# A two-layer hybrid network: eight stages of a layer written as three

## The chip, the cores and the metric

The kernel runs on one core of a Trainium2 chip. A core has a matrix engine (PE, its weight loads PEld), a vector engine (DVE), a scalar engine (ACT), a general engine (POOL) and a queue (SP) that issues transfers. The metric is the device time of one execution in microseconds, the median of the runs shown.

## What is computed

Two layers run over 640 tokens (512 latent, 128 of context) of width 1024. Of a layer, this is what the change touches:

```python
h = rmsnorm(x, lp['norm1_g']) * (1.0 + sc1) + sh1
proj = h @ lp['w_in']
r_a, k_a, v_a, q_b, k_b, v_b, x_c, g_c = jnp.split(proj, SPLIT_POINTS, axis=-1)
# differential attention: rotated queries and keys, then
o = rmsnorm(o, lp['diff_subln_g'], eps=1e-5) * (1.0 - lam_init)
# recurrence: its outputs' end
o = head_layernorm(o_sum, lp['rwkv_ln_g'].reshape(H_A, HD_A))
bonus = jnp.sum(rh * kh * lp['rwkv_rk'], axis=-1, keepdims=True) * vh
out = (o + bonus).reshape(B, T, W_A) * g
```

`sh1`, `sc1` and four more vectors come from a product of the condition with `mod_w`. Behind this follow the output projection and an expert stage, which the change leaves as they are, but for the place of the norm's squares.

## The kernel before, in words

Everything is fp32, with tokens along the free axis (`[128, chunk, 640]`). Large products split each operand into a high and a low part (`high` on ACT, `low` on DVE) and issue three matmuls (`split3`, L196 to L198). Each stage is an `nc.Block()`: each engine runs its own list in order, semaphores order them inside, and all engines meet at its end. Buffers live as long as the Python scope that holds them.

A layer's stages, in order: `load_stage` (the vectors' transfer L159, small products and exponentials); `mod_stage` (three small DVE steps, `mod_shifts`); `proj_gemm` (norm 1, then 21 columns of 128, with weights in a ring of three, PSUM in pairs of banks 0 to 5, and the linear recurrence on DVE and ACT beside it; banks 6 and 7 hold its gates); `vtok_stage` (values with tokens on the partitions: three pieces of 256 columns, five token tiles each, 15 groups of 24 matmuls, weights in one raw buffer and two split ones); `rope_stage` (eight rotations: PE permutes L871, POOL times cosine L881, DVE times sine L888 and adds L891; pieces 0 and 1 of the late modulation); `rwkv_prepare` (low-rank products L978, key norm, then four rounds of decays, and modulation pieces 2 to 7); `mix_stage` (the recurrence and the attention); `subln_stage`; `rwkv_finish`; then the output projection.

`Modulation` computes a vector piece from 2 MB of weights in two halves of a ring: `sums` (L346) and `turn` (L355) on PE, `take_row` (L363) and `take_columns` (L368) on ACT. It uses banks 5 to 7. In `rwkv_prepare` ACT handles two pieces ahead of each round's three exponentials (L1021 to L1024), on which DVE's round waits (L1063).

In `norm_programs` ACT writes squares (L456) into a ring of two, PE sums them (L479), DVE scales the sum (L484), ACT takes `Ln` and `Exp`, DVE multiplies (L494), ACT scales and makes the high part, and DVE the low one (L489). In `proj_gemm` DVE's three first `low` steps stand ahead of L484.

## Time and profile before

| | us |
|---|---|
| median of 3 runs | 4836.77 (4822.12 to 4838.63) |
| profiled execution, its own time | 4823.6 |
| its span in the profile | 4821.8 |
| matrix engine busy | 4173.8 (87%) |
| vector engine busy | 3557.3 (74%) |
| scalar engine busy | 1498.2 (31%) |
| general engine busy | 1304.8 (27%) |

The profile shows each engine's instructions with start and duration. Busy shares are means over all stages; since stages end at a common point, each is read by its own window. Clock is the granted share of the matrix engine's 2.4 GHz: 0.50 is 1.2 GHz.

### The profile page before, as it was taken

What the parts mean: (1) busy time and instruction counts of PE and PEld (TensorE: products, weight loads), DVE (VectorE), ACT (ScalarE), POOL (GpSimd) and SP (SyncE); (2) the same over time, 40 slices, a digit from 0 to 9 for tenths busy, and PEclk for the clock granted to TensorE, in tenths of its full rate; (3) what the DMA queues carried; (4) which work ended last, traced back from release to release, by engine and by line L of the source; (5) the groups of instructions that cost most, each with busy time, mean ns of one, the idle gap of its engine ahead of it and who ended that gap; (6) DMA issues with size and microseconds to landing.
All of it is one profiled execution on the core that took longest, in us unless ns stands there. A gap on an engine that the chain in (4) does not pass through costs nothing. (4 is left out here: it accounts for less than half of the span.)

```text
span 4821.8 us, 74006 instructions
## 1 busy us (share of the span) xinstructions
PE 4173.8 (87%) x28014; PEld 3382.9 (70%) x28014; DVE 3557.3 (74%) x6627; ACT 1498.2 (31%) x2206; POOL 1304.8 (27%) x1046
## 2 busy tenths in 40 slices
PE   6977996899878999999879689868996989999996
PEld 4955775875556878888768367768653777887885
DVE  2436654359997999999944466433799979999997
ACT  3323542311123333332242245223111333323333
POOL 0000000004302666655500000000133046656553
PEclk8977987999989999999989689789998999999998
DMA  5132001239968999999821400012587799999996
GB/s 210 49 123 74 2 2 37 88 95 321 300 181 301 409 408 408 403 406 404 327 70 58 161 5 2 2 51 81 190 302 239 225 350 408 408 408 405 404 407 230
DMA packets 402055, 1079.48 MB, mean 224 GB/s; under 512 B 37632, under 2 KB 177152, under 8 KB 395136
## 3 DMA queue, kind: packets, MB, share of 16 engines
q1 hardware_dynamic: 254336, 539.10, 31.7%
q0 software_dynamic: 147456, 536.94, 28.9%
q8 instruction: 157, 2.57, 0.2%
q14 instruction: 106, 0.87, 0.1%
HBM read 996.47 MB, written 79.43 MB: 223 GB/s over the span
## 5 line engine op out<-in xcount | busy, mean ns | idle before, releaser
L1641 POOL DMA_INDIRECT ring<-peer_u_rows,rows x512 | 630.1, 1231 | 2446.2 <-DVEq L1882 1524.3
L1641 POOL DMA_INDIRECT ring<-peer_v,rows x512 | 652.4, 1274 | 432.0 <-DVE acc L2275 376.6
L196 PE MATMUL ps<-vhi,wlo 128*128 128x512 f32 x1536 | 619.3, 403 | 135.6 <-DVE wlo L2254 135.4
L1598 PE MATMUL ps<-h,u 128*128 128x384 f32 x2048 | 689.7, 495 | 26.1 <-ACT hh L1609 24.1
L2275 DVE SCALAR_TENSOR_TENSOR acc<-ring,act,acc 128x1024 f32<-128x1024 f32 x508 | 647.4, 1279 | 45.7 <-DMA ring<-peer_v,rows 39.4
L1645 DVE SCALAR_TENSOR_TENSOR ring<-ring,acc 128x1024 f32<-128x1024 f32 x512 | 623.3, 1223 | 38.9 <-DMA ring<-peer_u_rows,rows 32.2
L197 PE MATMUL ps<-vlo,whi 128*128 128x512 f32 x1536 | 613.0, 399 | 0.0
L198 PE MATMUL ps<-vhi,whi 128*128 128x512 f32 x1536 | 611.3, 398 | 0.0
L1598 PEld LDWEIGHTS ps<-h,u 128*128 128x128 f32 x2048 | 390.7, 194 | 288.8 <-issue 42.2
L196 PEld LDWEIGHTS ps<-vhi,wlo 128*128 128x128 f32 x1536 | 297.0, 193 | 216.5 <-issue 142.7
L196 PE MATMUL ps<-xhi,ulo 128*128 128x384 f32 x1024 | 344.7, 337 | 18.6 <-DVE xlo L2232 18.6
L198 PE MATMUL ps<-xhi,uhi 128*128 128x384 f32 x1024 | 344.4, 336 | 0.0
L197 PE MATMUL ps<-xlo,uhi 128*128 128x384 f32 x1024 | 344.0, 336 | 0.0
L198 PEld LDWEIGHTS ps<-vhi,whi 128*128 128x128 f32 x1536 | 297.4, 194 | 64.2
L197 PEld LDWEIGHTS ps<-vlo,whi 128*128 128x128 f32 x1536 | 297.8, 194 | 61.0
L2240 DVE TENSOR_TENSOR vlo<-v,vhi 128x1024 fp32r<-128x1024 f32 x256 | 311.9, 1218 | 22.1 <-ACT vhi L2184 22.1
L2184 ACT ACTIVATE vhi<-v 128x1024 fp32r<-128x1024 f32 x256 | 269.5, 1053 | 160.3 <-DMA v<-peer_v 152.0
L2189 ACT ACTIVATE whi<-u 128x384 fp32r<-128x384 f32 x128 | 66.8, 523 | 692.4 <-DVE u L2249 674.2
L1609 ACT ACTIVATE hh<-ps 128x384 f32<-128x384 f32 x256 | 122.3, 480 | 425.7 <-PE ps L1598 372.9
L196 PE MATMUL ps<-hhi,proj_lo 128*128 128x320 f32 x672 | 211.5, 315 | 22.4 <-DVE hlo L489 21.0
L197 PE MATMUL ps<-hlo,proj_hi 128*128 128x320 f32 x672 | 209.4, 312 | 0.0
L198 PE MATMUL ps<-hhi,proj_hi 128*128 128x320 f32 x672 | 209.4, 312 | 0.0
(362 smaller groups left out, 8046.1 us busy)
## 6 DMA issues: line engine op xcount, KB each, us to landing
u<-peer_u SPq DMA_DIRECT2D x256, 512.0 KB
v<-peer_v SPq DMA_DIRECT2D x256, 512.0 KB
...
mod_ring<-mod_late SPq DMA_DIRECT2D x32, 1024.0 KB, 5.1
hidden<-hh SPq DMA_DIRECT2D x128, 192.0 KB
u<-hidden SPq DMA_DIRECT2D x128, 192.0 KB
...
```

Of the source, the lines that this page charges most:

```text
L196: pe.matmul(out, lhs[1], rhs[0], start=start, stop=False)
L197: pe.matmul(out, lhs[0], rhs[1], start=False, stop=False)
L198: return pe.matmul(out, lhs[0], rhs[0], start=False, stop=stop)
L1598: mm = pe.matmul(self.g.ps[:, bank, 0:ND], self.u[:, slot, kc, :], self.x[:, kc, 0:ND], start=(kc == 0), stop=(kc == KC - 1))
L1609: return self.g.nc.scalar.activation(self.hh[:, slot, :], self.g.ps[:, slot, 0:ND], ACT.Gelu)
L1641: return pool.indirect_dma_start(to, None, table, rows)
L1645: return ve.scalar_tensor_tensor(row, row, 1.0, self.acc[:, x, :], ALU.mult, ALU.mult, accum_out=self.act[x][:, slot:slot + 1])
L2184: nc.scalar.activation(v2[0][:, j, :], v[:, j % 2, :], ACT.Copy).then_inc(v_hi, 1)
L2189: nc.scalar.activation(w2[0][:, j, :], h, ACT.Copy).then_inc(w_hi, 1)
L2240: ve.tensor_tensor(v2[1][:, j, :], v[:, j % 2, :], v2[0][:, j, :].bitcast(F32), ALU.subtract).then_inc(v_lo, 1)
L2275: ve.scalar_tensor_tensor(acc, r, w, acc, ALU.mult, ALU.add).then_inc(used, 1)
```

## The change

`load_stage`, `mod_stage`, `proj_gemm`, `vtok_stage` and `rope_stage` become one block, `proj_stage`. The squares go to eight chunks of `g.proj`; ACT writes them first, ahead of the vectors' small steps. The weight ring has four slots, and the value weights run through it as six more columns, two slots to a group, so that the moving operand of a value matmul is two pieces of 128 columns. Value sums use banks 0 to 5, rotations banks 6 and 7; a rotation follows each of groups 2 to 9. `rwkv_prepare` takes modulation pieces 0 to 4 with a ring of four halves, the caches' loads and the stores of new keys and values, and two copies on ACT. `subln_stage` and `rwkv_finish` become `mix_finish`, with pieces 5 to 7 behind their sums. The query stage's and the last norm's squares also get eight chunks.

```diff
+class LayerVectors:
...
+    def shifts(self, ve):
+        g = self.g
+        self.c = Counter(ve, self.done)
+        ve.wait_ge(self.loaded, 16)
+        mod_shifts(g, self.c, g.modE[:, bass.ds(self.l * 2 * KC, 2 * KC), :], 0, 2 * KC, (0, "n1", 1))
...
+    def exps(self, act):
+        g, nc = self.g, self.g.nc
+        act.wait_ge(self.loaded, 16)
+        act.wait_ge(self.done, 7)
+        nc.scalar.activation(g.tiny[:, 2:4], g.tiny[:, 0:2], ACT.Exp).then_inc(self.ex, 1)
+        nc.scalar.activation(g.nsp2[:, :], self.v("lam"), ACT.Exp, scale=-1.0).then_inc(self.lam_exp, 1)
+        act.wait_ge(self.lam_exp, 1)
+        nc.scalar.activation(g.nsp[:, :], g.nsp2[:, :], ACT.Ln, bias=1.0).then_inc(self.sp, 1)
...
-            if kc >= 2:
-                act.wait_ge(sum_ready, kc - 1)
-            nc.scalar.activation(sq[:, kc % 2, :], g.xT[:, kc, :], ACT.Square).then_inc(sq_ready, 1)
+            nc.scalar.activation(squares[:, kc, :], g.xT[:, kc, :], ACT.Square).then_inc(sq_ready, 1)
...
+W_RING = 4
...
+def proj_stage(g, l):
+    nc, d, R, W = g.nc, g.dram, PROJ_RING, W_RING
+    NV = VTOK // VP
...
+        def value_slots(i):
+            pair = sorted((NPROJ + 2 * i + j) % W for j in range(2))
+            return pair, slice(pair[0], pair[1] + 1, pair[1] - pair[0])
...
+        def slot_free(eng, n):
+            if n >= NPROJ + W:
+                eng.wait_ge(vt_ready, TILES * ((n - W - NPROJ) // 2 + 1))
+            elif n >= W:
+                eng.wait_ge(ready, n - W + 1)
...
+            pool.wait_ge(loaded, 32)
+            pool.wait_ge(taken, NPROJ)
+            for c in range(ROPE):
+                if c >= 2:
+                    pool.wait_ge(added, c - 1)
+                pool.tensor_tensor(tmp[:, 0, c % 2, :], g.proj[:, Q0 + c, 0:NS], cs[:, 0, :], ALU.mult).then_inc(cosd, 1)
...
+            vectors.load(sync)
+            for n in range(NW):
+                if n >= W:
+                    sync.wait_ge(w_lo, n - W + 1)
+                sync.dma_start(raw[:, n % W, :, :], weights(n)).then_inc(w_in[n % W], 16)
+                if n == W - 1:
                     lru.load(sync)
+                    at = CI["cos"][0]
+                    sync.dma_start(cs[:, :, :], d["consts"][:, at:at + 2 * NS]).then_inc(loaded, 16)
+                    sync.dma_start(perm[:, :], d["consts"][:, CI["perm"][0]:CI["perm"][0] + P]).then_inc(loaded, 16)
...
+            high(R)
+            vectors.exps(act)
             for n in range(NPROJ):
-                lru.on_scalar(act, n, taken)
-                if n + R < NPROJ:
-                    high(n + R)
+                lru.on_scalar(act, n, taken, vectors)
+                high(n + W)
+            for n in range(NPROJ + W, NW):
+                high(n)
...
+            def rotate(c):
+                if c == 0:
+                    pe.wait_ge(loaded, 32)
+                    pe.wait_ge(taken, NPROJ)
+                if c >= 2:
+                    pe.wait_ge(sind, c - 1)
+                pe.matmul(g.ps[:, 2 * R + c % 2, :], perm[:, :], g.proj[:, Q0 + c, 0:NS], start=True, stop=True).then_inc(rot, 1)
+            for i in range(NV):
+                pe.wait_ge(w_lo, NPROJ + 2 * i + 2)
+                at = value_slots(i)[1]
+                for t in range(TILES):
+                    n = i * TILES + t
+                    bank = n % (2 * R)
+                    if n < 2 * R:
+                        pe.wait_ge(taken, NPROJ - R + bank // 2 + 1)
+                    else:
+                        pe.wait_ge(vt_taken, n - 2 * R + 1)
+                    out = g.ps[:, bank, 0:VP].rearrange("p (a n) -> p a n", n=P)
+                    for kc in range(KC):
+                        mm = split3(pe, out, [x[:, kc, t * P:(t + 1) * P] for x in g.h2], [x[:, at, kc, :] for x in (hi, lo)],
+                                    start=(kc == 0), stop=(kc == KC - 1))
+                    mm.then_inc(vt_ready, 1)
+                    if 2 <= n < 2 + ROPE:
+                        rotate(n - 2)
...
+            vectors.shifts(ve)
             for n in range(R):
                 low(n)
+            vectors.products(ve)
             norm["vector"](ve)
+            low(R)
             for n in range(NPROJ):
                 ve.wait_ge(ready, n + 1)
                 if PROJ_ORDER[n] in range(Q0 + 2, X0):
                     k.wait()
                 ve.tensor_copy(g.proj[:, PROJ_ORDER[n], :].rearrange("p (h n) -> p h n", n=H2),
                                g.ps[:, 2 * (n % R):2 * (n % R) + 2, 0:H2]).then_inc(taken, 1)
-                if n + R < NPROJ:
-                    low(n + R)
+                low(n + W)
...
+                if n == 1:
+                    vectors.scalars(ve)
...
+            ve.wait_ge(taken, NPROJ)
             ve.tensor_scalar(g.proj[:, Q0:B0, NS:NT], g.proj[:, Q0:B0, NS:NT], DK ** -0.5, None, ALU.mult)
+            for n in range(NV * TILES):
+                i, t = divmod(n, TILES)
+                ve.wait_ge(vt_ready, n + 1)
+                ve.tensor_copy(g.vtok[:, t, i * VP:(i + 1) * VP], g.ps[:, n % (2 * R), 0:VP]).then_inc(vt_taken, 1)
+                if n in (TILES, TILES + 1):
+                    low(NPROJ + W + n - TILES)
+                if 2 <= n < 2 + ROPE:
+                    rotated(n - 2)
...
-def rope_stage(g, l, mod, rope):
...
-            mod.load(sync, range(1))
-            sync.dma_start(g.kctx[:, :, :], d["cache_k"][l]).then_inc(caches, 16)
-            sync.dma_start(g.vctx[:, :, :], d["cache_v"][l]).then_inc(caches, 16)
-            sync.dma_start(d["new_v"][l], g.vtok[:, TILES - 1, 256:VTOK]).then_inc(out_done, 16)
-            sync.dma_start(d["new_k"][l], g.proj[:, B0:B0 + CB, NS:NT]).then_inc(out_done, 16)
-            mod.load(sync, range(1, ROPE_MODS + 1))
...
+MODS_FIRST = 5
...
-        lw = g.sb(st, "lw", [P, 4, NT])
+        lw = g.proj[:, X0:X0 + 4, :]
...
-            mod.load(sync, range(ROPE_MODS + 1, NLATE))
+            mod.load(sync, range(2))
+            sync.dma_start(g.kctx[:, :, :], d["cache_k"][l]).then_inc(caches, 16)
+            sync.dma_start(g.vctx[:, :, :], d["cache_v"][l]).then_inc(caches, 16)
+            mod.load(sync, range(2, MODS_FIRST))
+            sync.dma_start(d["new_v"][l], g.vtok[:, TILES - 1, 256:VTOK]).then_inc(out_done, 16)
+            sync.dma_start(d["new_k"][l], g.proj[:, B0:B0 + CB, NS:NT]).then_inc(out_done, 16)
...
-                mod.on_scalar(act, ROPE_MODS + 2 * i)
-                mod.on_scalar(act, ROPE_MODS + 2 * i + 1)
+                for n in ((), (0, 1), (2, 3), (4,))[i]:
+                    mod.on_scalar(act, n)
...
+        mod = Modulation(g, st, lambda i: g.dram["mod_late"][l, MODS_FIRST + i], g.modL[:, MODS_FIRST * MP // P:, :], NLATE - MODS_FIRST, 4, "last_mod")
...
+            mod.load(sync, range(NLATE - MODS_FIRST))
...
+            def sum_heads(n, src):
+                if n >= 2:
+                    pe.wait_ge(taken, n - 1)
+                for bank, (a, b) in enumerate(((0, NS), (NS, NT))):
+                    mm = pe.matmul(g.ps[:, 2 * (n % 2) + bank, 0:b - a], g.bones, src[:, a:b], start=True, stop=True)
+                mm.then_inc(sums, 1)
+            for c in range(CA):
+                sum_heads(MEANS + c, g.outT[:, c, :])
+            for c in range(CB + CA):
+                pe.wait_ge(sq, c + 1)
+                sum_heads(SQUARES + c, s[:, c, :])
+            for c in range(CA):
+                pe.wait_ge(bonus, c + 1)
+                sum_heads(BONUS + c, bo[:, c, :])
+            for i in range(mod.n + 1):
+                mod.on_tensor(pe, i)
...
+            for c in range(CB):
+                nc.scalar.activation(s[:, c, :], g.outT[:, CA + c, :], ACT.Square).then_inc(sq, 1)
             for c in range(CA):
-                act.wait_ge(taken, 3 + c)
-                nc.scalar.activation(s2[:, c, :], g.outT[:, c, :], ACT.Square).then_inc(sq, 1)
-            for c in range(CA):
-                act.wait_ge(taken, 5 + c)
-                nc.scalar.activation(s2[:, c, :], s2[:, c, :], ACT.Ln).then_inc(logs, 1)
-            for c in range(CA):
+                act.wait_ge(taken, MEANS + c + 1)
+                nc.scalar.activation(s[:, CB + c, :], g.outT[:, c, :], ACT.Square).then_inc(sq, 1)
+            for c in range(CB + CA):
+                act.wait_ge(taken, SQUARES + c + 1)
+                nc.scalar.activation(s[:, c, :], s[:, c, :], ACT.Ln).then_inc(logs, 1)
+            for c in range(CB + CA):
                 act.wait_ge(logs, c + 1)
-                nc.scalar.activation(s2[:, c, :], s2[:, c, :], ACT.Exp, scale=-0.5).then_inc(roots, 1)
+                nc.scalar.activation(s[:, c, :], s[:, c, :], ACT.Exp, scale=-0.5).then_inc(roots, 1)
+            for i in range(mod.n + 1):
+                mod.on_scalar(act, i)
...
+            for c in range(CA):
+                ve.wait_ge(sums, MEANS + c + 1)
+                ve.scalar_tensor_tensor(g.outT[:, c, :], flat(MEANS + c), -1.0 / HD, g.outT[:, c, :], ALU.mult, ALU.add).then_inc(taken, 1)
             for c in range(CA):
                 ve.scalar_tensor_tensor(bo[:, c, :], g.proj[:, R0 + c, :], v("rk", c, c + 1), g.proj[:, K0 + c, :],
+                                        ALU.mult, ALU.mult).then_inc(bonus, 1)
+            for c in range(CB + CA):
+                ve.wait_ge(sums, SQUARES + c + 1)
+                ve.tensor_scalar(s[:, c, :], flat(SQUARES + c), 1.0 / HD, SUB_EPS if c < CB else GN_EPS, ALU.mult, ALU.add).then_inc(taken, 1)
             for c in range(CA):
+                ve.wait_ge(sums, BONUS + c + 1)
+                ve.tensor_tensor(bo[:, c, :], flat(BONUS + c), g.proj[:, V0 + c, :], ALU.mult).then_inc(taken, 1)
+            for c in range(CB):
+                ve.wait_ge(roots, c + 1)
+                k.did(ve.scalar_tensor_tensor(g.outT[:, CA + c, :], g.outT[:, CA + c, :], g.lam[:, 3:4], s[:, c, :],
+                                              ALU.mult, ALU.mult))
+            ve.wait_ge(taken, BONUS + CA)
             for c in range(CA):
+                ve.wait_ge(roots, CB + c + 1)
+                k.did(ve.scalar_tensor_tensor(g.outT[:, c, :], g.outT[:, c, :], v("lng", c, c + 1), s[:, CB + c, :], ALU.mult, ALU.mult))
+            k.wait()
             for c in range(CA):
+                k.did(ve.tensor_tensor(g.outT[:, c, :], g.outT[:, c, :], bo[:, c, :], ALU.add))
+            k.wait()
             for c in range(CA):
                 k.did(ve.tensor_tensor(g.outT[:, c, :], g.outT[:, c, :], gt[:, c, :], ALU.mult))
+            ve.wait_ge(mod.taken, mod.n)
+            mod_shifts(g, Counter(ve, late), g.modL[:, :, :], 2 * KC, 4 * KC, (1, "n2", 4))
...
-            load_stage(g, l)
-            mod_stage(g, l)
...
+                        mod = Modulation(g, s3, lambda i: dram["mod_late"][l, i], g.modL, MODS_FIRST, 4)
                         rwkv_prepare(g, l, keep, mod)
                     mix_stage(g, l, keep)
-                    subln_stage(g)
-                    rwkv_finish(g, keep)
+                    mix_finish(g, l, keep)
```

On ACT, the head of a layer, before (`tiny`, `nsp`: small vectors; `sq`: squares):

```order
L2399 UNCONDITIONAL_BRANCH [waits barrier_Pool_Activation_PE_DVE_SP_release]
L183 UNCONDITIONAL_BRANCH
L188 ACT_TABLE_LOAD [waits lambda_steps]
L188 ACTIVATE tiny_7<-tiny_7 128x2 [waits vectors_loaded]
...
L191 ACT_TABLE_LOAD
L191 ACTIVATE nsp_10<-nsp2_11 128x4 [waits lru_lambda_exp]
L156 UNCONDITIONAL_BRANCH
L709 UNCONDITIONAL_BRANCH [waits barrier_Pool_Activation_PE_DVE_SP_release]
L456 ACTIVATE sq_24<-xT_1 128x640 x2
L456 ACTIVATE sq_24<-xT_1 128x640 [waits norm1_summed] x6
```

And now:

```order
L2376 UNCONDITIONAL_BRANCH [waits barrier_Pool_Activation_PE_DVE_SP_release]
L746 UNCONDITIONAL_BRANCH
L448 ACT_TABLE_LOAD
L448 ACTIVATE proj_18<-xT_1 128x640 x8
L751 ACTIVATE proj_hi_25<-proj_raw_24 128x1024 [waits proj_w_loaded0]
...
L453 ACT_TABLE_LOAD
L453 ACTIVATE rs_23<-rs_23 128x640 [waits norm1_steps]
L455 ACT_TABLE_LOAD
```

Two barriers and the small exponentials no longer stand ahead of the squares; a table load does.

On PE, from the last value product to the end of the rotation stage, before (`wvh`, `wvl`: value weights; `perm`: permutation; `mod_ring`: modulation weights):

```order
L198 MATMUL ps<-wvh_33,hhi_22 128x256
L780 UNCONDITIONAL_BRANCH
L865 UNCONDITIONAL_BRANCH [waits barrier_Pool_Activation_PE_DVE_SP_release]
L871 MATMUL ps<-proj_18,perm_21 128x512 [waits rope_consts_loaded]
...
L871 MATMUL ps<-proj_18,perm_21 128x512 [waits sin_done] x4
L346 MATMUL ps<-mod_ring_41,scond_5 32x512 [waits mod_w_loaded0]
...
L871 MATMUL ps<-proj_18,perm_21 128x512 [waits sin_done] x2
L346 MATMUL ps<-mod_ring_41,scond_5 32x512 [waits mod_w_loaded0]
...
L355 MATMUL ps<-groups_6,mod_rows_42 128x2 [waits mod_row_taken]
...
L844 UNCONDITIONAL_BRANCH
```

And now, from the last projection column through the first value groups:

```order
L201 MATMUL ps<-hhi_20,proj_hi_25 128x320
L199 MATMUL ps<-proj_hi_25,hlo_21 128x256 [waits proj_sums_taken,proj_w_low]
...
L199 MATMUL ps<-proj_hi_25,hlo_21 128x256 [waits proj_sums_taken]
...
L201 MATMUL ps<-proj_hi_25,hhi_20 128x256
L798 MATMUL ps<-proj_18,perm_28 128x512 [waits proj_sums_taken,rope_consts_loaded]
L199 MATMUL ps<-proj_hi_25,hlo_21 128x256 [waits proj_sums_taken]
```

The value products follow the columns with no barrier, a permutation stands between two groups, and the modulation's rows are gone from here.

On ACT, in `rwkv_prepare` from the key norm's `Exp` on, before (`outT` holds the exponentials):

```order
L1016 ACTIVATE outT_35<-outT_35 128x640 [waits rwkv_key_logs] x2
L363 ACTIVATE mod_rows_42<-ps 128x512 [waits mod_transposed,mod_halves_used]
L368 ACTIVATE modL_14<-ps 128x8 [waits mod_transposed]
...
L1021 ACTIVATE outT_35<-outT_35 128x640 [waits rwkv_logs_ready]
L1023 ACTIVATE outT_35<-outT_35 128x640 [waits rwkv_exps_ready]
L1024 ACTIVATE outT_35<-outT_35 128x640
L363 ACTIVATE mod_rows_42<-ps 128x512 [waits mod_transposed,mod_halves_used]
```

And now:

```order
L961 ACTIVATE outT_31<-outT_31 128x640 [waits rwkv_key_logs] x2
L966 ACTIVATE outT_31<-outT_31 128x640 [waits rwkv_logs_ready]
L968 ACTIVATE outT_31<-outT_31 128x640 [waits rwkv_exps_ready]
L969 ACTIVATE outT_31<-outT_31 128x640
L366 ACTIVATE mod_rows_38<-ps 128x512 [waits mod_halves_used] x2
L371 ACTIVATE modL_14<-ps 128x8 [waits mod_transposed]
L966 ACTIVATE outT_31<-outT_31 128x640 [waits rwkv_logs_ready]
L968 ACTIVATE outT_31<-outT_31 128x640 [waits rwkv_exps_ready]
L969 ACTIVATE outT_31<-outT_31 128x640
L366 ACTIVATE mod_rows_38<-ps 128x512 [waits mod_transposed,mod_halves_used]
```

The first round's exponentials stand ahead of any modulation step.

## Rows read from the trace of the kernel before

**Rows 1.** The page's first line: span and instructions.

```profile
span 4821.8 us, 74006 instructions
```

**Rows 2.** Busy time by stretch: length, PE, PEld, DVE, ACT, POOL; clock, DMA, GB/s.

```profile
61.00:83.60 22.60, 11.42 (x32) 6.12 (x32) 6.70 (x8) 14.22 (x19) 0.89 (x1) 0.73 0.49 152
...
243.20:254.30 11.10, 0.00 (x0) 0.00 (x0) 2.92 (x2) 1.91 (x1) 0.00 (x0) 0.70 0.29 94
...
299.40:324.00 24.60, 15.86 (x56) 5.07 (x56) 15.16 (x18) 2.75 (x6) 10.10 (x8) 0.84 0.80 283
...
324.00:406.10 82.10, 52.92 (x200) 24.98 (x200) 38.12 (x49) 29.62 (x45) 0.00 (x0) 0.56 0.42 152
```

**Rows 3.** Timeline, head of layer 0: start, us, what ran, idle before.

```profile
52.67 0.36 SPq L159 DMA_DIRECT2D vec<-vecs  x1
...
60.96 1.36 ACT L456 ACTIVATE sq<-xT 128x640 f32<-128x640 f32 x2 [2.05 <-PEq L435]
...
77.76 1.28 ACT L463 ACT_TABLE_LOAD   x1
...
76.16 0.81 DVE L484 TENSOR_SCALAR rs<-ps 128x640 f32<-128x640 f32 x1
...
83.66 0.61 PE L196 MATMUL ps<-hhi,proj_lo 128*128 128x320 f32 x1 [10.49 <-DVE hlo L489]
```

**Rows 4.** Timeline, from the last projection column to the first value product.

```profile
254.38 0.58 PE L196 MATMUL ps<-wvh,hlo 128*128 128x256 f32 x1 [11.39 <-DVE wvl L821]
```

**Rows 5.** Timeline, value products and rotation.

```profile
293.68 0.42 DVE L829 COPY vtok<-ps 128x256 f32<-128x256 f32 x1 [2.46 <-PE ps L198]
...
303.93 1.25 DVE L891 SCALAR_TENSOR_TENSOR proj<-ropetmp 128x512 f32<-128x512 f32 x1
...
303.94 1.12 PE L871 MATMUL ps<-proj,perm 128*128 128x512 f32 x2 [0.76 <-DVE ropetmp L888]
```

**Rows 6.** Timeline, two modulation operations, then the preparation, layer 0.

```profile
319.77 1.94 PE L346 MATMUL ps<-mod_ring,scond 128*32 128x512 f32 x8 [0.50 <-DMA mod_ring<-mod_late]
...
321.64 1.87 PE L355 MATMUL ps<-groups,mod_rows 128*128 128x2 f32 x8
...
330.30 1.22 PE L978 MATMUL ps<-proj,wB 64*128 64x512 f32 x1 [6.79 <-DMA scan<-consts]
...
366.96 0.83 DVE L1063 TENSOR_TENSOR ar<-proj,outT 128x640 f32<-128x640 f32 x1 [3.29 <-ACT outT L1024]
...
381.54 0.83 DVE L1063 TENSOR_TENSOR ar<-proj,outT 128x640 f32<-128x640 f32 x1 [6.65 <-ACT outT L1024]
...
394.71 0.83 DVE L1063 TENSOR_TENSOR ar<-proj,outT 128x640 f32<-128x640 f32 x1 [5.24 <-ACT outT L1024]
...
404.87 0.82 DVE L1071 TENSOR_TENSOR proj<-proj,outT 128x640 f32<-128x640 f32 x1
```

**Rows 7.** Timeline, from the mix's end to the output projection, layer 0.

```profile
767.79 2.61 ACT L916 ACTIVATE s<-outT 128x640 f32<-128x640 f32 x4 [17.57 <-PEq L1129]
...
778.46 2.62 ACT L922 ACTIVATE s<-s 128x640 f32<-128x640 f32 x4
...
802.32 1.36 ACT L511 ACTIVATE outhi<-outT 128x640 fp32r<-128x640 f32 x2 [4.89 <-PEq L1501]
```

**Rows 8.** Timeline, four marks of layer 1.

```profile
2418.53 0.35 SPq L159 DMA_DIRECT2D vec<-vecs  x1
...
2450.04 0.61 PE L196 MATMUL ps<-hhi,proj_lo 128*128 128x320 f32 x1 [10.49 <-DVE hlo L489]
...
2690.37 0.33 SPq L963 DMA_DIRECT2D wB<-rwkv_B  x1
...
2773.47 0.34 SPq L1175 DMA_DIRECT2D mask<-consts  x1
```

**Rows 9.** DMA issues: transfers, KB each, median us from issue to landing.

```profile
mod_ring<-mod_late SPq DMA_DIRECT2D x32, 1024.0 KB, 5.1
```

**Rows 10.** One line's instructions: a moving operand of two pieces of 64 columns.

```profile
L1200 PE MATMUL ps<-ar,proj x640: 269/414/473, 410.8 to 3109.0; 64*64 64x128 f32 x160
```

323 lines of the change are left out of this document (90 added, 233 removed).

## The prediction

> **What bounds the kernel now.** The profiled span is 4821.8 us [rows 1], and its own time 4823.6; the median of the runs shown is 4836.8. All sums below are differences inside the one profiled execution, taken off the median. I read busy time by stretch first, since stages end at common points and a share over the whole span says nothing of one of them. Then I read the timeline of each stretch in which the matrix engine (PE) idles, to see which engine's step ends the wait.
>
> Four stretches of a layer matter, and in each something other than a full engine sets the time. At the head PE is busy 11.42 of 22.6 us; between the projection's end and the first value product it does nothing for 11.1 us; the rotation stage lasts 24.6 us for 15.9 us of PE work that is cheap elsewhere; the preparation lasts 82.1 us with PE at a granted clock of 0.56 and the vector engine (DVE) busy 38.1 us [rows 2]. Between them the projection keeps PE full, and the mix, the output projection and the expert stage are not touched. Stages are in a row, so what a stage loses is taken from the end. This is the main reason to let the parts add up.
>
> **Part 1, the head.** Before, the vectors' transfer is issued at 52.67 and the squares start at 60.96, two stages later; the sum's scaling by DVE starts at 76.16 and the first matmul at 83.66 [rows 3]. Now the squares' stage begins where the vectors' did, at 52.6. The order of ACT has a table load first, 1.28 us by the load at 77.76 [rows 3], so the squares start at 53.9 and PE's sums 0.7 later. They take the 11.42 us of [rows 2] and end at 66.0: PE was the bound there, so dropping the ring of two gives nothing. Before, they ended at 73.2 and the scaling waited 3 us more for DVE's three `low` steps. Those now need ACT's squares (5.4, at half of the 1.36 of a pair each) and three `high` steps and end near 64, the small products included, so they are covered by the sums. The scaling starts at 66.1, the chain to the first matmul keeps its 7.5 us (76.16 to 83.66), and the matmul starts at 73.6: **10.0 us** saved. In layer 1 the same distance, from 2418.53 to 2450.04, is 31.5 us [rows 8] against 31.0 in layer 0; with 20.9 us now it saves **10.6**. The three vector steps that DVE makes first wait for the vectors' transfer, and behind them stand only the `low` steps, which are not ready then. The softplus and the lambda steps lie behind the norm, where ACT and DVE idle; they cost nothing unless the first gate comes, four columns later.
>
> The trace shows the `Exp` starting right behind its table load, at 1.28 us after it [rows 3]. The Trainium skill, on the page "ScalarE: Activation LUTs", section "What ACT_TABLE_LOAD costs", adds a drain to the load and gives about 2.66 us for a switch. By the page the head would save 1.4 us less in each layer and the time would be 2.8 us higher; the row decides.
>
> **Part 2, from the first matmul to the preparation.** It takes 240.3 us in both layers (83.66 to 324.0; 2450.04 to 2690.37) [rows 2, 3, 8]. The gap of 11.39 us ahead of the value products [rows 4] is the wait for a transfer that could only be issued in its own stage. In the new order the six value columns are in the ring while columns 17 to 20 run, ACT's `high` and DVE's `low` step of each having a whole column's time, so the gap goes. What is left is PE: 159.5 us to the projection's end, 15 groups at 2.88 (0.42 busy and 2.46 idle for one DVE copy between two) [rows 5] is 43.2, and eight permutations. One takes 1.12 us alone, its drain included [rows 5]; among other matmuls I take 0.9, so 7.2 in all. With 0.9 for the barrier that is 210.8: **29.5 us** saved in each layer. The gap also made the first value products run at 1.2 GHz; I count that inside the 45.1 us they took against 43.2.
>
> The cover of the rotation is DVE and POOL. For a group with a rotation DVE has 0.42 for the copy, 1.25 for the sum and about 0.7 for the sine step (what is left of the 1.88 of a rotation, below) [rows 5], 2.4 us, against PE's 3.8; two groups get a `low` step of 1.2 more, still under PE's. Six banks give slack. If the cover fails, a rotation costs the 1.88 us it took alone (1.12 and 0.76 idle) [rows 5] instead of 0.9: 8 us a layer (8 x 1.0). Below nothing it can't go, as the permutations are issued either way.
>
> The moving operand in two pieces is not in the trace for this data type. The nearest row is the pair product with two pieces of 64 columns at a median of 414 ns [rows 10] with an eightfold smaller tile, fp32; nothing in it speaks of a penalty. I take none; the bound above is the rival below.
>
> **Part 3, the preparation.** Its first product stands 6.3 us behind the stage's start, waiting for a transfer that queues behind modulation weights issued in the rotation stage [rows 6]. Now nothing is ahead; for 1 MB I take 5.2 us, the 5.1 of a 1 MB piece [rows 9], so 1.1 us goes. Two copies more on ACT end before the first sum is there. Then DVE's rounds wait for ACT's exponentials: 3.29, 6.65 and 5.24 us, 15.2 in all [rows 6]. ACT is idle but stands behind modulation steps, which wait for PE. In the new order no such step is ahead of the first exponentials, two pieces each are ahead of the next two, and one of the last. What is late next? At the low clock PE needs 1.94 for half a piece and 1.87 for its turn [rows 6], so about 5.6 a piece; two pieces, 11.2, come against 7.9 of a DVE round, but they have been prepared ahead by the ring of four. Following the lists step by step, the second and third exponentials end within 0.5 us of DVE's need, so I take 0.5 off: 14.7. DVE is then the bound. With the transfer, **15.8 us**; layer 1's stage was 83.1 instead of 82.1 [rows 2, 8], so **16.8** there. New stores wait on SP for the fourth piece's ring slots, but end long before DVE.
>
> **Part 4, the finish.** From the first square to the output projection's first step are 34.5 us (767.79 to 802.32) [rows 7], two passes of squares, sums, `Ln`, table load, `Exp` and product. Now one: ten sums at the pace of [rows 2] (11.42 for eight) end near 14.5, the last `Ln` is at 14.3, the table load 1.28 and six `Exp` at 0.66 [rows 7] end at 19.6, and DVE would end at 24.7. Next late is the modulation, which ACT can serve only from 19.6: copies of two rows, 1.2; turn, 1 to 1.9; the third piece's sums, whose second half lands near 23 (slot free at 16.6, and 5.1 [rows 9] with its forerunner ahead), 1 to 2 us a half; two turns; three shifts. That ends between 27.8 and 31.2 with the barrier, by the clock. I take 28.8: **5.7 us** in each layer. Ends: 9.4 if the modulation were hidden, nothing if the sums and `Exp` did not overlap.
>
> **Sum.** Layer 0: 10.0 + 29.5 + 15.8 + 5.7 = 61.0. Layer 1: 10.6 + 29.5 + 16.8 + 5.7 = 62.6. Together 123.6 us, so 4836.8 - 123.6 = **4713 us**. The squares of the other two norms are PE-bound as here: 0.
>
> **Rivals.** *The covers fail in part*: DVE falls behind in the value groups (8 us a layer) and ACT still gates the rounds (half of 15.2) because PE stays at 1.2 GHz through the pieces: 2 x 15.5 on top, 4744. For it speaks that DVE's sum takes 1.25 us while POOL runs and that the exponentials are nearly late; against it, that DVE has 1.4 us of slack a group.
>
> *The low-rank sums run at the high clock.* PE was granted 0.50 at their start, having idled 6.8 us [rows 6]. Now it comes from 210 us of full work and idles 0.9 + 5.2 = 6.1. If the clock held, PE's share of some 20 us would near half: 10 us a layer, 4693. The 11.1 us gap, with a mean of 0.70 [rows 2], shows that it falls somewhere inside such an idle stretch, so this is the less likely.
>
> *Slower: the two-piece moving operand costs.* 360 value matmuls a layer now take 120 ns each (2.88 by 24). If a jump between pieces halted the stream so that they took four times that, it would be 130 us a layer: 4713 + 259 = 4972. It turns the change to a loss from 120 + 123.6/720 x 1000 = 292 ns a matmul. Nothing in the trace speaks for it.
>
> *It doesn't do what it says*: value weights late in spite of the ring, the gap back: 2 x 11.4, 4736, inside the range.
>
> **How the numbers follow.** Forecast 0.68, covers fail 0.15 (the last rival with it), high clock 0.12, slower 0.03, a loss of the whole gain to something unseen 0.02. The range reaches from the high-clock case with a lower level of runs (before ran from 4822 to 4839), 4680, to the failed covers, 4748. Faster by over 0.5% (24 us, about what a measurement tells from no change) 0.95, within 0.5% 0.02, slower 0.03.
>
> **What would show it.** Right: the first projection matmul 21 us behind the vectors' transfer; no idle PE between projection and value products; permutations about 0.9 us apart from their groups' 2.88; the preparation near 66 us with DVE waits under 1 us; the finish near 29 us, with a modulation step last. Wrong: value matmuls over 120 ns; DVE copies late by more than a group; the rounds still waiting for ACT; PE's clock at 1.00 in the low-rank sums.

## The result

Both kernels were timed side by side four times: 4837.7 us before (4822.12 to 4849.3) and 4710.5 us after (4709.56 to 4713.48), a ratio of 0.9738, 95% interval 0.972 to 0.9755. The forecast was 4713, in a range of 4680 to 4748. The saving by the medians is 127.2 us, 123.6 forecast; by the two profiled executions it is 114.0 (4821.8 in [rows 1] less 4707.8). The page's first line of the kernel after:

```profile
span 4707.8 us, 73952 instructions
```

A total hides which steps came out. So each layer is cut at the same marks in every execution: the vectors' transfer, the first projection matmul, the issue of `wB`, the issue of `mask`, the first squares of the finish (ACT), the first transfer of `w_out`, and from there to the next layer or the end. Both kernels were profiled a second time (in two of the runs below). Lengths in us:

| | head | to preparation | preparation | mix | finish | rest |
|---|---|---|---|---|---|---|
| before, layer 0 | 31.0 | 240.5 | 82.1 | 361.6 | 34.9 | 1615.8 |
| before again, layer 0 | 30.1 | 239.0 | 83.8 | 367.0 | 35.2 | 1616.5 |
| after, layer 0 | 20.7 | 208.9 | 67.0 | 366.0 | 32.2 | 1615.8 |
| after again, layer 0 | 21.4 | 209.2 | 67.1 | 373.1 | 33.0 | 1615.8 |
| before, layer 1 | 31.5 | 240.3 | 83.1 | 369.4 | 35.3 | 1643.6 |
| before again, layer 1 | 31.2 | 241.0 | 81.7 | 370.0 | 35.4 | 1646.0 |
| after, layer 1 | 20.7 | 209.0 | 66.7 | 370.4 | 30.8 | 1646.5 |
| after again, layer 1 | 20.5 | 210.3 | 65.9 | 368.8 | 32.9 | 1642.5 |

The means of two profiles each give these savings per layer: head 9.5 us in layer 0 and 10.8 in layer 1, to the preparation 30.7 and 31.0, preparation 15.9 and 16.1, finish 2.5 and 3.5. That is 58.6 and 61.4, 120.0 in all; 61.0 and 62.6 were forecast. The 114.0 of the first pair holds a mix that was 4.4 us longer in layer 0 and a rest 2.9 longer in layer 1. The change leaves the mix alone, and of the rest it touches only the squares of two norms; in the means of two profiles the rest keeps its length within 0.4 us.

**Head.** The timeline of the kernel after, as in [rows 3]: start, length, what ran, idle before.

```profile
52.86 1.28 ACT L448 ACT_TABLE_LOAD   x1 [0.74 <-PEq L127]
...
53.07 0.36 SPq L160 DMA_DIRECT2D vec<-vecs  x1
...
54.15 5.12 ACT L448 ACTIVATE proj<-xT 128x640 f32<-128x640 f32 x8
54.94 11.21 PE L471 MATMUL ps<-proj,keep 128*128 128x512 f32 x32 [3.04 <-ACT proj L448]
...
66.27 0.82 DVE L476 TENSOR_SCALAR rs<-ps 128x640 f32<-128x640 f32 x1 [1.67 <-PE ps L471]
...
73.77 0.60 PE L199 MATMUL ps<-hhi,proj_lo 128*128 128x320 f32 x1 [7.61 <-DVE hlo L481]
```

The squares start 1.1 us behind the vectors' issue instead of 8.3, PE's sums set the time to 66.2, and DVE, free again, waits 1.67 us for them. The matmul stands 20.7 us behind the transfer.

**Values.** DVE's and POOL's timeline around one rotation, and the row of all permutations (durations ns, min, median, max):

```profile
247.94 0.42 DVE L856 COPY vtok<-ps 128x256 f32<-128x256 f32 x1 [1.45 <-PE ps L201]
248.80 0.69 DVE L829 SCALAR_TENSOR_TENSOR ropetmp<-ps,ropecs 128x512 f32<-128x512 f32 x1 [0.44 <-PE ps L798]
249.53 0.69 DVE L832 SCALAR_TENSOR_TENSOR proj<-ropetmp 128x512 f32<-128x512 f32 x1
251.67 0.42 DVE L856 COPY vtok<-ps 128x256 f32<-128x256 f32 x1 [1.45 <-PE ps L201]
...
250.30 1.30 POOL L730 TENSOR_TENSOR ropetmp<-proj,ropecs 128x512 f32<-128x512 f32 x1 [2.44 <-DVE proj L832]
...
L798 PE MATMUL ps<-proj,perm x32: 590/592/594, 240.3 to 2577.5; 128*128 128x512 f32 x32
```

A group with a rotation takes 3.73 us from copy to copy, 2.88 for the group and 0.85 for the permutation. DVE waits for PE twice in it, so the cover holds. The sum takes 0.69 us where it took 1.25 [rows 5], and POOL's step now runs while DVE is idle (250.30 to 251.60, between the sum and the next copy).

**Preparation.** The first product and the four rounds' first steps, as in [rows 6]:

```profile
289.27 14.84 PE L920 MATMUL ps<-proj,wB 64*128 64x512 f32 x32 [7.48 <-DMA scan<-consts]
...
322.46 0.82 DVE L1009 TENSOR_TENSOR ar<-proj,outT 128x640 f32<-128x640 f32 x1
...
330.31 0.82 DVE L1009 TENSOR_TENSOR ar<-proj,outT 128x640 f32<-128x640 f32 x1
...
338.15 0.82 DVE L1009 TENSOR_TENSOR ar<-proj,outT 128x640 f32<-128x640 f32 x1
...
343.66 0.82 DVE L1009 TENSOR_TENSOR ar<-proj,outT 128x640 f32<-128x640 f32 x1
```

No round waits for ACT any more. The first product still waits for the transfers, 6.7 us behind ACT's first step of the stage at 282.53. From the issue of `wB` (282.65) it is 6.6 us, and it was 6.2 before (324.12 to 330.30): here nothing was saved.

**Finish.** PE's modulation and what stands behind it, as in [rows 7]:

```profile
715.64 2.61 ACT L1486 ACTIVATE s<-outT 128x640 f32<-128x640 f32 x4 [17.28 <-PEq L1075]
...
737.12 1.06 PE L349 MATMUL ps<-mod_ring,scond 128*32 128x512 f32 x8 [0.39 <-DMA mod_ring<-mod_late]
...
740.08 1.93 PE L349 MATMUL ps<-mod_ring,scond 128*32 128x512 f32 x8 [1.90 <-DMA mod_ring<-mod_late]
741.94 1.78 PEld L358 LDWEIGHTS ps<-groups,mod_rows 128*128 128x128 f32 x8 [1.66 <-issue]
741.94 1.87 PE L358 MATMUL ps<-groups,mod_rows 128*128 128x2 f32 x8
...
746.25 0.23 DVE L428 TENSOR_TENSOR modT<-modL,vec 128x64 f32<-128x64 f32 x1 [6.16 <-ACT modL L371]
...
747.47 2.62 ACT L503 ACTIVATE outhi<-outT 128x640 fp32r<-128x640 f32 x4 [1.25 <-PEq L1453]
```

From first to last row it is 31.8 us, and 28.8 were forecast. DVE has ended its own chain at 740.1 and waits 6.16 us for the modulation: the last half of its weights comes late, and from there PE is at its slow pace, 1.93 and 1.87 us instead of 1.06 and 1.05.

### The profile page after: what moved, and what is told of

The parts are those of the page before. It is cut to its first block and busy times, and to the rows that moved or that the text cites. A ratio compares the mean times of both kernels' runs of the same rounds, so it can differ in the third digit from the quotient of the medians.

```text
span 4707.8 us, 73952 instructions
## 1 busy us (share of the span) xinstructions
PE 4159.8 (88%) x28014; PEld 3384.9 (72%) x28014; DVE 3554.3 (75%) x6633; ACT 1493.6 (32%) x2210; POOL 1329.6 (28%) x1046
## 5 line engine op out<-in xcount | busy, mean ns | idle before, releaser
L1618 POOL DMA_INDIRECT ring<-peer_v,rows x512 | 679.3, 1327 | 405.2 <-DVE acc L2252 336.1
L199 PE MATMUL ps<-hhi,proj_lo 128*128 128x320 f32 x672 | 210.5, 313 | 15.2 <-DVE hlo L481 15.2
L199 PEld LDWEIGHTS ps<-xhi,ulo 128*128 128x128 f32 x1024 | 193.4, 189 | 21.4 <-DVE xlo L2209 19.0
```

Of the source, the lines that this page charges most:

```text
L199: pe.matmul(out, lhs[1], rhs[0], start=start, stop=False)
L1618: return pool.indirect_dma_start(to, None, table, rows)
```

## Experiments

The theory is the prediction's: four separate savings, one for each stretch, each with the cause that it named. The rival for each is that something else in the same stretch saved the time; one part is undone at a time to tell. Three further runs take the preparation apart, and the last three look for what is left. Ratios are each to runs of the kernel before on the same chip. Its medians there were 4828 to 4841 us, so totals from different chips can't be told apart by a few us; such differences are read from the marks.

### The kernel after, again

No edit. 

> The changed kernel once more, unaltered, as the base of the other runs and to see how much one profiled execution differs from the next. The first comparison gave 114 us less by the two profiled spans and 127 us by the medians, and the mix, in which nothing was changed, was 4.3 us longer in layer 0 and 0.9 us longer in layer 1. Theory (the granted clock in the long stages differs from execution to execution): the head, the values, the preparation and the finish keep their lengths within 0.5 us (208.8 from first matmul to preparation, 67.0 for the preparation), while the mix moves by some us and the span with it; time within 10 us of 4710. Rival (the change makes the mix slower): the mix of layer 0 stays at 366 us and that of layer 1 at 370.

The time was 4713.1 us, ratio 0.9752 (0.9724 to 0.9779). The four changed stretches differ by up to 2.1 us from the first profile (the finish of layer 1), more than the 0.5 expected, while the mix of layer 0 went from 366.0 to 373.1. The rival is out: that mix isn't a constant of the kernel.

### The kernel before, again

No edit. 

> The kernel before once more, unaltered, for one more profiled execution of it. The first had a mix of 361.6 us in layer 0 and 369.4 in layer 1; five profiled executions of kernels with the change had 366.0 to 375.4 and 368.8 to 375.3. Theory (the granted clock in the mix differs from execution to execution, and the first profile of before was a good one): the mix of layer 0 is 366 us or more this time, the span 4830 to 4845. Rival (the change makes the mix slower, by where it puts things or by what PE did ahead of it): again 360 to 363 us in layer 0.

The time was 4831.2 us in one run, the span 4829.4, and the mix took 367.0 and 370.0 us. So the kernel before has such mixes too. Over the 12 profiled executions of kernels with the change the mix of layer 0 ran from 359.1 to 375.4. The first hundred us of its longest (the run with the old order on ACT) and its shortest (all pieces, new order), in the busy time by stretch (length, PE, PEld, DVE, ACT, POOL; clock, DMA, GB/s):

```profile
349.60:449.60 100.00, 89.24 (x1169) 69.55 (x1171) 58.36 (x116) 41.89 (x84) 0.00 (x0) 0.75 0.02 5
```

```profile
357.00:457.00 100.00, 86.42 (x1384) 67.93 (x1385) 67.46 (x134) 49.88 (x100) 0.00 (x0) 0.92 0.02 6
```

At a granted clock of 0.75 against 0.92 PE gets through 1169 matmuls instead of 1384. And the whole mix in the same two executions:

```profile
349.60:725.00 375.40, 333.86 (x4736) 264.96 (x4737) 220.81 (x484) 152.63 (x333) 0.00 (x0) 0.81 0.01 3
```

```profile
357.00:716.00 359.00, 314.48 (x4736) 250.67 (x4736) 220.80 (x484) 152.24 (x332) 0.00 (x0) 0.87 0.01 3
```

The matmuls are the same 4736, and DVE and ACT are as long busy; only PE's time differs, by 19 us, with the clock. The mixes of before, 361.6 and 369.4 us, have 0.85 and 0.83. Why the clock differs is open. The mix is where the executions differ most. With two profiles of before, a shift of its mean by a few us can't be excluded: in layer 0 it is 364.3 before and 369.6 for the twelve.

### Value weights asked for late

```
+                if n == NPROJ:
+                    sync.wait_ge(taken, NPROJ)
                 sync.dma_start(raw[:, n % W, :, :], weights(n)).then_inc(w_in[n % W], 16)
...
-                high(n + W)
+                if n + W < NPROJ:
+                    high(n + W)
...
+            for n in range(NPROJ, NPROJ + W):
+                low(n)
```

> One part undone: the value weights aren't asked for before the last projection column is taken, and their high and low steps stand behind it, in the same stage. Theory (what the join of the stages saves is the wait for that transfer): PE idles between the projection and the values again. Two slots of 0.5 MB (3.7 us to land), two high and one low step, about 1 us each: 7 to 9 us idle. With the first value products at the lower clock, 1 to 2 us more: 8 to 11 us a layer, 4726 to 4732 in all. Rival (the barrier and the loop of the old stage, not the transfer, made the gap): under 3 us a layer, below 4717.

The time was 4740.8 us, ratio 0.9813 (0.9784 to 0.9843): 27.7 us over the kernel after on the same chip, more than expected. From the first matmul to the preparation it takes 221.8 and 221.6 us, 12.3 a layer over the mean of the two profiles of after. PE's first value product:

```profile
241.43 0.58 PE L199 MATMUL ps<-proj_hi,hlo 128*128 128x256 f32 x1 [9.77 <-DVE proj_lo L827]
```

The idle time is 9.77 us, and the first product takes 0.58 for 0.28, so the first group is slow as well. The rival, under 3 us, is out: the gap comes back with no barrier in it. It holds the transfer, issued at 232.74 and followed by ACT's first `high` step at 237.25, and then some 4 us of `high` and `low` steps. Joining the stages pays because the ring can ask early and the split steps run under the columns.

### Rotations behind the values

```
-                    if 2 <= n < 2 + ROPE:
-                        rotate(n - 2)
+            for c in range(ROPE):
+                rotate(c)
...
-                if 2 <= n < 2 + ROPE:
-                    rotated(n - 2)
+            for c in range(ROPE):
+                rotated(c)
```

> One part undone: the eight rotations stand behind all value products instead of between them, on PE, DVE and POOL alike, in the same stage. Theory (the rotation is covered but for PE's own 0.85 us of each): behind the values PE and DVE alternate at 1.88 us each as before, 15 to 17 us in all, and the 6.8 between the products go; 8 to 10 us a layer more, 4727 to 4731. Rival (DVE's steps set the pace between the products as well, so that nothing was hidden): under 3 us a layer, below 4717.

The time was 4731.8 us, ratio 0.9794 (0.9768 to 0.9821), and the stretch takes 218.0 and 218.1 us: 8.7 a layer more, as expected. Rotations alone, in DVE's and PE's timeline:

```profile
280.41 1.26 DVE L832 SCALAR_TENSOR_TENSOR proj<-ropetmp 128x512 f32<-128x512 f32 x1
...
289.88 0.69 DVE L832 SCALAR_TENSOR_TENSOR proj<-ropetmp 128x512 f32<-128x512 f32 x1
...
280.44 1.12 PE L798 MATMUL ps<-proj,perm 128*128 128x512 f32 x2 [0.77 <-DVE ropetmp L829]
```

They come every 1.89 us, and the sum is back at 1.26, with POOL at work beside it (279.86 to 281.12). The last one, at 289.88, takes 0.69: POOL had ended at 288.7.

### The squares behind the vectors

```
+            vectors.exps(act)
             norm["scalar_first"](act)
...
-            vectors.exps(act)
```

and DVE's small products ahead of its first `low` steps. 

> One part undone: ACT makes the two exponentials and the softplus of the layer's vectors ahead of the squares, as in the kernel before, and so waits for the vectors' transfer and DVE's first steps; the stage is one block as in the changed kernel. Theory (the head gained by letting the squares start without the vectors): the squares start at about 8.3 us behind the transfer's issue, as before, for 1.1 now, so the head is 27 to 29 us long instead of 20.7, 6.5 to 8 us a layer, 4724 to 4728. Rival (the head gained by the barrier that fell away, and the vectors are hidden either way): under 2 us a layer, below 4715.

The time was 4725.6 us, ratio 0.9765 (0.9746 to 0.9785). The head is 26.0 and 27.5 us long, 5.3 and 6.8 more than 20.7, where 6.5 to 8 were expected:

```profile
56.47 1.28 ACT L179 ACT_TABLE_LOAD   x1 [4.83 <-DVE tiny L173]
...
58.08 1.28 ACT L182 ACT_TABLE_LOAD   x1
...
59.49 5.11 ACT L448 ACTIVATE proj<-xT 128x640 f32<-128x640 f32 x8
```

The squares start 6.9 us behind the vectors' issue, 8.3 before. Against the head of before, 30.1 to 31.5, another 3.7 to 5.0 us are still gone with this order. In layer 0 the squares start 1.4 us earlier than before, PE's sums take 10.74 for 11.42, and 3.0 are DVE's `low` steps, which no longer stand between the sums and the scaling. They end at 69.2, ahead of the sums, because ACT is through with the squares at 64.6: with eight chunks it waits for no sum. With the ring of two its last square ended at 71.8.

### The old order on ACT

```
-                for n in ((), (0, 1), (2, 3), (4,))[i]:
+                for n in ((0, 1), (2, 3), (4,), ())[i]:
```

> One part undone: ACT's modulation steps stand two pieces ahead of each exponential again, as in the kernel before, but for five pieces (0 and 1, then 2 and 3, then 4, then none). Theory (the order on ACT alone made DVE wait 14.7 us of its rounds): the first two exponentials come late by what PE needs for two pieces at its granted clock, 3 us and 6.7 us, and the third is late by up to 5 us; the preparation is 75 to 81 us long instead of 67, 8 to 14 us a layer, 4727 to 4739. Rival (the gain came from having fewer pieces in the stage, five for seven, and not from their place): under 3 us a layer, below 4717.

The time was 4718.9 us (4708.8 to 4722.3), ratio 0.9761 (0.9732 to 0.979); but the preparation is 66.4 and 66.5 us long, no longer than with the new order. The profiled execution was longer than that of the kernel after on this chip, but its mixes, 375.4 and 375.0 us, hold the difference. The one wait for ACT that is left:

```profile
330.29 0.82 DVE L1009 TENSOR_TENSOR ar<-proj,outT 128x640 f32<-128x640 f32 x1 [0.64 <-ACT outT L969]
```

This speaks against the prediction's reading of the 15.2 us. It had put them down to ACT's order and to PE's pace at the low clock, 5.6 us a piece. The timeline of PE and SP in the kernel before, in the same stage, shows a slower pace:

```profile
353.31 31.78 SPq L337 DMA_DIRECT2D mod_ring<-mod_late  x10
...
358.46 1.94 PE L346 MATMUL ps<-mod_ring,scond 128*32 128x512 f32 x8 [3.53 <-DMA mod_ring<-mod_late]
360.96 1.94 PE L346 MATMUL ps<-mod_ring,scond 128*32 128x512 f32 x8 [0.56 <-DMA mod_ring<-mod_late]
...
365.50 1.93 PE L346 MATMUL ps<-mod_ring,scond 128*32 128x512 f32 x8 [0.80 <-DMA mod_ring<-mod_late]
368.31 1.93 PE L346 MATMUL ps<-mod_ring,scond 128*32 128x512 f32 x8 [0.88 <-DMA mod_ring<-mod_late]
```

From 358.46 on, every half waits for its transfer. With a ring of two, a transfer is issued when the half two places ahead is used: 5.1 us to land [rows 9] and 1.93 to use make 7.0 us for two halves, and the trace has 7.04 (358.46 to 365.50) and 7.35 (360.96 to 368.31). Two halves are a piece, so the two pieces ahead of a round take over 14 us, against DVE's round of 7.9. The change doubled that ring. Three runs take this apart.

### A ring of two halves, new order

```
-                        mod = Modulation(g, s3, lambda i: dram["mod_late"][l, i], g.modL, MODS_FIRST, 4)
+                        mod = Modulation(g, s3, lambda i: dram["mod_late"][l, i], g.modL, MODS_FIRST, 2)
```

SP also asks for one piece ahead of the caches' loads instead of two.

> The changed kernel with a ring of two halves for the modulation weights in the preparation, as before, for four; the changed order on ACT is kept. The old order with a ring of four cost nothing with five pieces. What is left of the differences to the kernel before, whose rounds waited 15.2 us for ACT, is the ring: with two halves a half's transfer is only issued when the one two places ahead of it is used, and PE got one in 3.6 us there. Theory A (order and ring cover for each other, and either alone takes most of the waits): the third exponential, behind pieces 2 and 3, is some 2.5 us late, the fourth 1.5 more; the preparation is 70 to 73 us long, 3 to 6 us a layer more, 4717 to 4724. Theory B (the ring is the cause and the order does nothing): 10 us or more of waits, the preparation 77 us or longer, 4731 or more. Rival C (the order alone does it): under 68.5 us, below 4715.

The time was 4719.4 us, ratio 0.9775 (0.975 to 0.98), and the preparation takes 70.9 and 71.7 us. DVE's rounds:

```profile
329.56 0.82 DVE L1009 TENSOR_TENSOR ar<-proj,outT 128x640 f32<-128x640 f32 x1
...
339.82 0.83 DVE L1009 TENSOR_TENSOR ar<-proj,outT 128x640 f32<-128x640 f32 x1 [2.33 <-ACT outT L969]
...
347.96 0.83 DVE L1009 TENSOR_TENSOR ar<-proj,outT 128x640 f32<-128x640 f32 x1 [2.67 <-ACT outT L969]
```

This is theory A: order and ring cover for each other. With five pieces, the old order with the large ring waits 0.6 us, the new order with the small ring 5.0, and both new nothing. Layer 1 has 0.7, 4.9 and nothing. The fourth corner, both old, is the kernel before, with 15.2 (16.0 in layer 1); but it served one piece more, and two ahead of the third round instead of one, so it isn't quite the same case.

### All eight pieces in the preparation, old order and new

Both leave the finish without modulation (`MODS_FIRST` is 8). ACT's order is

```
(0, 1), (2, 3), (4, 5), (6, 7) ahead of the four exponentials
```

in the first and `(), (0, 1), (2, 3), (4,)` with 5 to 7 behind them in the second.

> All eight modulation pieces in the preparation and none in the finish, with ACT's steps two pieces ahead of each exponential, as before; the count and the order are now as in the kernel before, but the first two pieces are in the ring at the start. With five pieces the old order cost nothing (the preparation was 66.4 us long), so the place on ACT is not what made DVE wait. Theory (a piece that isn't in the ring comes at the pace of its transfer, 3.6 us a half, and only an order that puts it ahead of an exponential makes that a wait): the second to fourth exponential come later and later, the last one ends near 20 us behind its time, the preparation is 82 to 88 us long; the finish without modulation 25 to 26 us; 10 to 15 us a layer more, 4731 to 4741. Rival (it was PE's low clock and not the transfers; the ring's start is enough): below 4720.

> All eight pieces in the preparation and none in the finish, with the changed kernel's order for the first five and pieces 5 to 7 behind the last exponential on ACT. Theory: DVE waits for nothing, as its exponentials stand behind five pieces only, and the three others come at the pace of their transfers, some 8 us each behind DVE's end: the preparation is 73 to 79 us long, the finish 25 to 26; 1 to 5 us a layer more than the changed kernel, 4713 to 4721. It would show that the order matters where there are more pieces than the rounds can cover. Rival (count alone matters): as long as with the old order.

The times were 4713.0 and 4711.3 us, ratios 0.9756 (0.9739 to 0.9773) and 0.9751 (0.9736 to 0.9766). The preparation is 74.6 and 76.6 us long with the old order, well under the 82 to 88 expected, and 74.1 and 74.0 with the new one; the finish 25.9 to 26.0 in both. DVE's waits with the old order:

```profile
331.84 0.82 DVE L1009 TENSOR_TENSOR ar<-proj,outT 128x640 f32<-128x640 f32 x1 [1.30 <-ACT outT L969]
...
340.38 0.82 DVE L1009 TENSOR_TENSOR ar<-proj,outT 128x640 f32<-128x640 f32 x1 [0.60 <-ACT outT L969]
...
352.46 0.82 DVE L1009 TENSOR_TENSOR ar<-proj,outT 128x640 f32<-128x640 f32 x1 [6.61 <-ACT outT L969]
```

With the ring of four 8.5 us of waits are left of 15.2, with two pieces more to serve. The first three rounds stand behind two pieces each, as in the kernel before: they wait 0, 1.30 and 0.60 us, where it waited 3.29, 6.65 and 5.24 [rows 6]; in layer 1 it is 4.2 us in all for 16.0. This is the closest comparison of the two rings. The 6.61 us are the fourth round's, behind pieces 6 and 7, where the kernel before had none. With the new order DVE waits for nothing, but the last pieces outlast it: it is through at 349.0 and the stage at 356.9. So neither beats the other, and what the finish saves, the preparation pays.

### Six pieces first

`MODS_FIRST` is 6, and ACT takes `(4, 5)` ahead of the last exponential. 

> Six modulation pieces in the preparation and two in the finish, for five and three; ACT takes the sixth ahead of the last exponential, with the fifth. Theory (the finish ends with the third piece's transfer, whose halves have to wait for ring slots: PE waits for them until 740.08 of a stage that ends at 747.5; the preparation has room, as its last piece is done 6.6 us ahead of DVE): the finish is then set by DVE's chain, which ends at 740.1, and lasts 26 to 27.5 us instead of 32; the preparation is 0 to 2 us longer. 3.5 to 6 us a layer less, 4698 to 4705. Rival (the finish is set by PE's low clock in its turns, or the preparation becomes late by as much): within 1 us a layer of 4711.

The time was 4708.8 us, ratio 0.9731 (0.9706 to 0.9757). The stages do as expected, the finish 25.9 us in both layers, the preparation 67.9; the mix of 373.3 in layer 0 takes part of it back in the profiled run. Expected were 4698 to 4705; its four runs spread from 4702 to 4722, and the total alone shows no gain. The end of the finish:

```profile
743.78 1.05 PE L358 MATMUL ps<-groups,mod_rows 128*128 128x2 f32 x8 [1.45 <-ACT mod_rows L366]
...
746.64 1.56 DVE L1527 TENSOR_TENSOR outT<-outT,gt 128x640 f32<-128x640 f32 x2
...
748.12 0.22 DVE L428 TENSOR_TENSOR modT<-modL,vec 128x64 f32<-128x64 f32 x1
```

DVE goes from its last product to the shifts without a wait, though two turns still stand at the end. So the third piece was what the finish waited for, the only one whose halves had to wait for ring slots. The run takes away its transfer, sums and turn together, and its turns were at PE's fast pace; how much each was worth isn't shown.

### The first low-rank weights ahead

```
+            sync.dma_start(g.wb[:, :, :], d["rwkv_B"][l]).then_inc(early, 16)
+            sync.wait_ge(early, 16)
             lru.store(sync)
...
-            pe.wait_ge(loaded, 48)
...
+            pe.wait_ge(loaded, 32)
             for c in range(CA):
                 sums(gb[:, c * P:(c + 1) * P], g.proj[:, LG, :])
```

> The low-rank weights of the first eight sums are loaded in the projection's stage (one tile, 0.25 MB), and PE waits for the third weight and DVE for the scan's mask only where they are needed. Theory (the preparation's start waits for nothing but this transfer): the first product stands 1 us behind the stage's start instead of 6.7, so the stage is 5 to 6 us shorter, 10 to 12 us in all, 4699 to 4701. If PE also keeps its higher clock, having idled for 2 us only, the eight sums go at 0.65 instead of 1.22 us a matmul and the low-rank sums, which all steps of DVE wait for, end up to 8 us earlier again: 4685 to 4695. Rival (something else is late behind it, DVE's own squares or ACT's tables): under 2 us a layer, above 4707.

The time was 4706.8 us, ratio 0.9725 (0.9706 to 0.9744): a smaller gain than either theory had. From the first matmul to the mix it is 272.9 and 273.4 us, 275.9 and 275.7 in the kernel after, so 2.3 to 2.9 us a layer, little more than the rival's two. The wait has a new owner, of the kind that the rival named:

```profile
286.34 14.83 PE L920 MATMUL ps<-proj,wB 64*128 64x512 f32 x32 [4.88 <-ACT proj L942]
```

`Tanh` and `Sigmoid` of the inputs, with a table load each, stood right behind the transfer, and after 4.9 us of idling PE still ran slowly.

### The three edits together

Six pieces first, the weights ahead, and

```
             for n in range(NPROJ + W, NW):
                 high(n)
+            act.wait_ge(taken, NPROJ)
+            nc.scalar.activation(g.proj[:, LW, :], g.proj[:, LW, :], ACT.Tanh).then_inc(early, 1)
+            nc.scalar.activation(g.proj[:, LG, :], g.proj[:, LG, :], ACT.Sigmoid).then_inc(early, 1)
+            act.wait_ge(early, 2)
```

in `proj_stage`. 

> Three edits together: six modulation pieces in the preparation (ACT takes 4 and 5 ahead of the last exponential), the low-rank weights of the first eight sums loaded in the projection's stage, and the Tanh and Sigmoid of their inputs made by ACT there too, behind the last high step. With the second alone PE still idled 4.9 us, for ACT's table load and these two steps, and then ran at 1.22 us a matmul. Now nothing is left to wait for but the barrier. Theory A (PE's clock falls with an idle stretch of some us, so an idle of about 1 us keeps it): the low-rank sums take some 12 us for 21.6, the preparation is 13 us shorter less 1 for the sixth piece, the finish 6 shorter, 18 us a layer, 4672 to 4680. Theory B (the clock falls at the stage's change whatever the idle, or soon behind it with these small products): 1.22 us a matmul again, 5 us from the start and 5 from finish and sixth piece, 10 us a layer, 4688 to 4694.

The time was 4687.2 us (4679.6 to 4698.2, five runs), ratio 0.9699 (0.9681 to 0.9717): faster than both kernels, and between the two theories. The finish is 25.9 us in both layers; from first matmul to mix it is 264.5 in layer 0 and 270.8 in layer 1. PE's first product in each:

```profile
283.30 9.14 PE L924 MATMUL ps<-proj,wB 64*128 64x512 f32 x32 [0.79 <-PEq L687]
```

```profile
2578.29 13.38 PE L924 MATMUL ps<-proj,wB 64*128 64x512 f32 x32 [0.79 <-PEq L687]
```

and the clock in the busy time by stretch:

```profile
281.00:296.00 15.00, 14.21 (x58) 8.50 (x57) 3.14 (x6) 9.57 (x13) 0.00 (x0) 1.00 0.78 300
```

```profile
2578.30:2582.00 3.70, 3.70 (x10) 1.85 (x11) 2.66 (x4) 2.92 (x4) 0.00 (x0) 0.84 0.68 179
2582.00:2590.00 8.00, 8.00 (x20) 5.05 (x19) 0.00 (x0) 3.60 (x5) 0.00 (x0) 0.50 1.02 425
```

It is theory A in layer 0 and theory B in layer 1, after the same idle stretch of 0.79 us. In layer 1 the clock was still up in the first 3.7 us and fell while PE was busy without a gap, so the idle stretch alone doesn't decide. What does is open.

## Why the prediction held, and where it did not

**Head: right.** It took 20.7 us against 20.9 (21.4 in one layer of the second profile), with PE's sums as the bound and DVE's `low` steps covered. The squares' wait is 5.3 to 6.8 us of the 10 when it alone is undone. One sentence was wrong, "dropping the ring of two gives nothing": it holds for PE's sums, but the squares' eight chunks are what lets ACT reach the `high` steps early, and so what covers the 3 us of `low` steps that the same paragraph counts. The table load shows no drain: it starts at 52.86 and is 1.28 us long, and the squares start at 54.15. The Trainium skill ("ScalarE: Activation LUTs", "What ACT_TABLE_LOAD costs") adds one; the trace disagrees, at this place as behind the load of [rows 3], from 77.76 to the `Exp` at 79.06.

**To the preparation: right, with 1.2 to 1.5 us a layer more saved than forecast.** The gap went, and the groups of 2.88 and the permutations (0.85 for 0.9) came as counted; gap and cover, undone one by one, cost 12.3 and 8.7 us a layer. That is 21.0 of 30.9. The other 9.9 no run undoes; the barriers, the old rotation stage's start and its modulation operations fell away as well, and the rest is put down to them by argument alone. That the cover can't fail was argued from DVE's slack; the slack was larger than computed, since the sum fell to 0.69 us.

**Preparation: the size was right (16.0 for 16.3 us, mean of the layers), the cause was not, and that is luck.** The step that failed is "ACT is idle but stands behind modulation steps, which wait for PE": it ends the chain at PE. PE itself waited for its weights: a ring of two halves gave it a piece every 7.0 to 7.4 us. ACT's order passed that on to DVE. The sum gave the 14.7 to the order and used the ring only to keep the later exponentials in time. With five pieces the old order with the new ring waits 0.6 us and the new order with the old ring 5.0: the ring takes nearly all of it without the order, and the order most of it without the ring. With eight pieces, the new ring and the old order the same three rounds wait 1.9 us in layer 0 and 4.2 in layer 1, for 15.2 and 16.0. The transfer's term failed too: 5.2 us were put for 5.7, from the issue of `scan` at 283.56 to the first product, with four halves in the queues right behind it, and of the 1.1 that it was to save nothing came (6.2 us from the issue of `wB` before, 6.6 now).

**Finish: the mechanism was right, the size was not.** A saving of 5.7 us was forecast and 2.5 and 3.5 were measured. The lengths between first squares and output projection, 30.5 to 32.7 in four layers of two profiles, lie above the stated range of 27.8 to 31.2 in three of the four. The term that was mis-sized is the third piece: its second half was put near 23 us and came at 24.4 (740.08), and behind it all operations ran at the slow pace: 1.93, 1.87 and a second turn of 1.84. In layer 1 of the same profile the half came at 25.1, but the turns took 1.05 and 1.02, and the stretch is the one of 30.5. A piece fewer took 6 us off.

**The sum.** By the marks the four parts saved 20.3, 61.7, 32.0 and 6.0 us in the two layers together, for 20.6, 59.0, 32.6 and 11.4 forecast. The finish was 5.4 too high and the stretch to the preparation 2.7 too low, so that the total is within 4 us is in part luck.

**The rivals.** The covers did not fail. The two-piece moving operand costs nothing: 2.88 us a group of 24, 120 ns each, as before. The high clock in the low-rank sums was rightly thought unlikely in this kernel, with 7.5 us of idling ahead of them; where that was cut to 0.79 it came in layer 0 and was lost within 4 us in layer 1.
